# A mixture-of-experts stage in which each pair of experts shares one rest of 32 rows

## The reference

```python
g_sel = jnp.argmax(p_grp, axis=-1)
top_p, top_e = lax.top_k(jax.nn.softmax(le_sel, axis=-1), TOP_K)      # TOP_K = 2
e_idx = g_sel[:, None] * E_PER_GROUP + top_e
def expert_rows(args):
    xb, e = args
    return (jax.nn.silu(xb @ w_e_gate[e]) * (xb @ w_e_up[e])) @ w_e_down[e]
contrib = ys[dest].astype(jnp.float32) * w_flat[order][:, None]
return jax.ops.segment_sum(contrib, tok_sorted, num_segments=T)
```

## Time and profile before

| | us |
|---|---|
| median of the runs | 2455.64 (2447.79 to 2460.75) |
| profiled execution, its own time | 2455.0 |
| its span on the core | 2455.0 |
| PE busy | 2273.7 (93%) |
| PEld busy | 1570.4 (64%) |
| DVE busy | 1204.2 (49%) |
| ACT busy | 822.2 (33%) |
| POOL busy | 119.8 (5%) |
| HBM read and written | 384.10 MB and 16.83 MB, 163 GB/s over the span |

### The profile page before, as it was taken

How to read it: one execution, slowest core, us unless ns; L and a number is a source line. 1 busy time by engine, 2 the same in 40 slices (tenths; PEclk the granted TensorE clock), 3 DMA queues, 4 the chain that set the end, 5 groups by cost and what they waited for, 6 DMA issues and landing times.

```text
span 2455.0 us, 29702 instructions
## 1 busy us (share of the span) xinstructions
PE 2273.7 (93%) x11726; PEld 1570.4 (64%) x11726; DVE 1204.2 (49%) x1761; ACT 822.2 (33%) x1255; POOL 119.8 (5%) x160
## 2 busy tenths in 40 slices
PE   6999998679999999978997689999999889999997
PEld 3788756423333333346777677888887777888885
DVE  3799576400000000047756543877824473877922
ACT  3322453311111111135474164332424273323422
POOL 0000000021111111100003000000000000000000
PEclk8999999889999999988999589999999899999999
DMA  8442204539999999831120011222222301222221
GB/s 354 184 170 77 82 15 191 220 122 380 385 381 382 389 388 389 324 143 69 69 102 2 1 35 69 103 103 103 103 103 80 127 1 69 103 92 83 99 103 69
DMA packets 36406, 384.56 MB, mean 157 GB/s; under 512 B 10080, under 2 KB 10336, under 8 KB 13408
## 3 DMA queue, kind: packets, MB, share of 16 engines
q1 hardware_dynamic: 27520, 374.91, 39.1%
q0 software_dynamic: 8800, 8.45, 1.0%
HBM read 384.10 MB, written 16.83 MB: 163 GB/s over the span
## 4 chain that ended last, share of the span: by engine, by line
PE 69%; DVE 5%; ACT 3%; issue 1%; DMA 1%; POOL 0%; SPq 0%; DVEq 0%; ACTq 0%; POOLq 0%
PE PS L616 14%; PE PS L618 14%; PE PS L617 14%; PE PS L818 9%; PE PS L857 5%; PE PS L838 5%; PE PS L865 2%; PE PS L988 1%; PE PS L808 1%; PE PS L576 1%; PE PS L1181 0%; PE PS L903 0%; DVE A L1812 0%; DVE A L2412 0%; DMA A<-y_assignments 0%
## 5 line engine op out<-in xcount | busy, mean ns | idle before, releaser
L616 PE MATMUL PS<-h_hi_r,w_hi_r 128*128 128x512 f32 x1056 | 425.1, 403 | 11.8 <-DVE A L1812 5.0
L617 PE MATMUL PS<-h_r,w_hi_r 128*128 128x512 f32 x1104 | 433.8, 393 | 0.0
L618 PE MATMUL PS<-h_hi_r,ring_r 128*128 128x512 f32 x1056 | 414.5, 392 | 0.0
L2084 DVE TENSOR_TENSOR ring_r<-ring,w_hi_r 128x1024 fp32r<-128x1024 f32 x196 | 238.7, 1222 | 341.6 <-ACT w_hi_r L1424 341.5
L1424 ACT ACTIVATE w_hi_r<-ring 128x1024 fp32r<-128x1024 f32 x196 | 206.1, 1057 | 462.7 <-PE PS L618 292.0
L616 PEld LDWEIGHTS PS<-h_hi_r,w_hi_r 128*128 128x128 f32 x1056 | 200.5, 190 | 66.6 <-issue 12.7
L617 PEld LDWEIGHTS PS<-h_r,w_hi_r 128*128 128x128 f32 x1104 | 210.2, 190 | 47.3 <-issue 4.8
L618 PEld LDWEIGHTS PS<-h_hi_r,ring_r 128*128 128x128 f32 x1056 | 200.5, 190 | 42.7
L2073 DVE TENSOR_TENSOR A<-A,PS 128x512 f32<-128x512 f32 x16 | 11.0, 688 | 395.9 <-PE PS L818 395.9
L818 PE MATMUL PS<-A 128*64 128x512 f32 x768 | 170.2, 600 | 0.1
L1812 DVE SCALAR_TENSOR_TENSOR A<-A,vec 128x511 f32<-128x511 f32 (+15 forms) x216 | 160.1, 741 | 6.7
(11 more groups left out here) (463 smaller groups left out, 3622.5 us busy)
## 6 DMA issues: line engine op xcount, KB each, us to landing
A<-wexp SPq DMA_DIRECT2D x64, 2048.0 KB, 9.4
ring<-wall SPq DMA_DIRECT2D x63, 2048.0 KB, 8.0
ring<-wexp SPq DMA_DIRECT2D x16, 2048.0 KB, 17.0
h<-wexp SPq DMA_DIRECT2D x16, 2048.0 KB, 13.3
A<-wada SPq DMA_DIRECT2D x12, 2048.0 KB, 15.8
x<-xt_in SPq DMA_DIRECT2D x2, 2048.0 KB, 11.6
A<-y_assignments SPq DMA_DIRECT2D x4, 1024.0 KB, 8.0
h_tokens<-A SPq DMA_DIRECT2D x4, 512.0 KB, 2.8
```

Of the source, the lines that this page charges most:

```text
L616: mm(out, w[0], x_[0], start=first, stop=False)
L617: mm(out, w[0], x_[1], start=False, stop=False)
L618: return mm(out, w[1], x_[0], start=False, stop=last_)
L2084: tt(ring_r[:, slot, :, cols], ring[:, slot, :, cols], w_hi_r[:, :, cols].bitcast(F32), ALU.subtract).then_inc(S("w_lo"), 1)
```

## The change

Per pair there is now one rest of 32 rows instead of two. It belongs to the expert of the pair with more rows; the kernel works out from the counts which one that is and puts it first (`place` in the routing, a table `blki` that is no longer the identity). So the first expert of a pair has room for 96 rows, the second for 64. In the first two pairs (FIXED) the order stays, because their gates are loaded before the counts are known. A pair has 160 slots instead of 192, and the additional pairs hold 160 rows of one expert.

The rest's products keep their number, and each has 256 columns: the four column groups of the array take (gate, up) x (half of the 512 columns) of the one expert for gate and up, and a quarter of the 1024 output columns each for down. Gate and up use columns 0 to 255 of PSUM bank 5, down columns 256 to 511. The hidden rest is 64 partitions (two halves) x 256, and is turned in two transposes. The results leave PSUM in four copies of 32x256.

On the SP queue the loop now reads six experts at its head, and per pair it issues ups(p) and gates(p+1) together at the end of the rest of gate and up of p-1, and downs(p) at the end of the rest of down of p-1. The last downs are issued behind the loop, when the copies of the last pair but one are done.

```diff
-PAIR_ROWS = 2 * CAP
+PAIR_ROWS = 2 * HALF + QUARTER
+FIXED = 2
-MORE = 2 * T // (CAP + 1)
+MORE = 2 * (2 * T // (CAP + 1 + HALF + 1))
...
-                for q in range(2):
-                    es = [expert(2 * d + q, j) for j in range(2)]
-                    rwait(sp, S("m_pc"), 2 * PRODUCTS * d + m_done(q - 2, 2))
-                    for j in range(2):
-                        gate_of(q, j, es[j])
-                    rwait(sp, S("m_pc"), 2 * PRODUCTS * d + m_done(q - 1, 2))
-                    for j in range(2):
-                        up_of(j, es[j])
-                    rwait(sp, S("m_pc"), 2 * PRODUCTS * d + m_done(q - 1, 4))
-                    for j in range(2):
-                        down_of(j, es[j])
+                done = 2 * PRODUCTS * d
+                before, first, second = experts(2 * d - 1), experts(2 * d), experts(2 * d + 1)
+                gates(0, first)
+                rwait(sp, S("m_pc"), done + m_done(-2, 4))
+                downs(before)
+                rwait(sp, S("m_pc"), done + m_done(-1, 2))
+                ups(first)
+                gates(1, second)
+                rwait(sp, S("m_pc"), done + m_done(-1, 4))
+                downs(first)
+                rwait(sp, S("m_pc"), done + m_done(0, 2))
+                ups(second)
+            rwait(sp, S("m_y1"), 2 * n)
+            downs(experts(2 * n - 1))
...
-                        for part, w in enumerate((moe_gate[q], moe_up)):
-                            for j in range(2):
-                                r = HALF * part + QUARTER * j
-                                last = mm(PS[r:r + QUARTER, 5, :], x_rest[:, k * HALF + QUARTER * j:k * HALF + QUARTER * (j + 1)], w[j][:, k, :],
-                                          start=k == 0, stop=k == KD - 1)
+                        for t in range(4):
+                            w = (moe_gate[q], moe_up)[t // 2][0]
+                            last = mm(PS[QUARTER * t:QUARTER * (t + 1), 5, 0:256], x_rest[:, k * QUARTER:(k + 1) * QUARTER],
+                                      w[:, k, 256 * (t % 2):256 * (t % 2 + 1)], start=k == 0, stop=k == KD - 1)
...
-                    pe.wait_ge(S("m_h"), 4 * d + (2 * q + 2))
-                    for k in range(4):
-                        last = nc.tensor.transpose(PS[:, 4, k * P:(k + 1) * P], A[:, 48, k * P:(k + 1) * P], ident)
+                    rwait(pe, S("m_h"), 4 * d + (2 * q + 2))
+                    for k in range(2):
+                        last = nc.tensor.transpose(PS[:, 4, k * HALF:(k + 1) * HALF], hid_rest[:, k * P:(k + 1) * P], ident[0:HALF, 0:HALF])
...
-                        for half in range(2):
-                            for j in range(2):
-                                r = HALF * half + QUARTER * j
-                                last = mm(PS[r:r + QUARTER, 5, :], hT_rest[:, k * HALF + QUARTER * j:k * HALF + QUARTER * (j + 1)],
-                                          moe_dn[j][:, 4 * half + k, :], start=k == 0, stop=k == 3)
+                        at = HALF * (k % 2) + QUARTER * (k // 2)
+                        for t in range(4):
+                            last = mm(PS[QUARTER * t:QUARTER * (t + 1), 5, 256:512], hT_rest[:, at:at + QUARTER],
+                                      moe_dn[0][:, 4 * (t // 2) + k, 256 * (t % 2):256 * (t % 2 + 1)], start=k == 0, stop=k == 3)
...
-                    for half in range(2):
-                        last = a_(yb[1][:, half, :], PS[HALF * half:HALF * (half + 1), 5, :], ACT.Copy)
+                    for t in range(4):
+                        last = a_(yb[1][:, t // 2, 256 * (t % 2):256 * (t % 2 + 1)], PS[QUARTER * t:QUARTER * (t + 1), 5, 256:512], ACT.Copy)
...
-            link(ts(er[1], er[0], float(CAP), None, ALU.is_gt))
-            for rows_in in range(CAP + PAIR_ROWS, T, PAIR_ROWS):
-                link(stt(er[1], er[0], float(rows_in), er[1], ALU.is_gt, ALU.add))
+            link(tt(place[:, :, 0], count[:, :, 1], count[:, :, 0], ALU.is_gt))
+            link(nc.vector.memset(place[:, 0:FIXED, 0], 0.0))
+            link(ts(place[:, :, 1], place[:, :, 0], -1.0, 1.0, ALU.mult, ALU.add))
+            link(ts(er[6], er[2], -float(QUARTER), float(CAP), ALU.mult, ALU.add))
+            link(tt(er[7], er[0], er[6], ALU.subtract))
+            link(ts(er[1], er[7], 0.0, None, ALU.is_gt))
+            for rows_in in range(PAIR_ROWS, T - HALF, PAIR_ROWS):
+                link(stt(er[1], er[7], float(rows_in), er[1], ALU.is_gt, ALU.add))
...
+            link(stt(er[5], er[2], -float(QUARTER), er[5], ALU.mult, ALU.add))
+            link(stt(er[3], er[2], float(HALF), C("slot0"), ALU.mult, ALU.add))
-            link(tt(asg[3], rank, by_expert(C("slot0")), ALU.add))
-            link(stt(asg[4], rank, float(HALF), by_expert(C("slot1")), ALU.is_ge, ALU.mult))
+            link(tt(asg[3], rank, by_expert(er[3]), ALU.add))
+            link(ts(asg[4], rank, float(HALF), float(HALF), ALU.is_ge, ALU.mult))
             link(tt(asg[3], asg[3], asg[4], ALU.add))
-            link(stt(asg[4], rank, float(CAP), by_expert(er[5]), ALU.is_ge, ALU.mult))
+            link(tt(asg[4], rank, by_expert(er[6]), ALU.is_ge))
+            link(tt(asg[4], asg[4], by_expert(er[5]), ALU.mult))
...
-            rows_of = (P, HALF)
+            rows_of = (P, QUARTER)
```

More of the change, by code:

```diff
@@ L73 @@
 CONSTS = [("ident", P), ("ones", P), ("after", P), ("tri_strict", P), ("tri_incl", P),
-          ("iota4", NG), ("iota8", EPG), ("iotab", MORE), ("iotae", E), ("slot0", E), ("slot1", E), ("slot2", E)]
+          ("iota4", NG), ("iota8", EPG), ("iotab", MORE), ("iotap", E), ("slot0", E), ("slot2", E)]
 COFF, NCST = {}, 0
@@ L240, in build @@
         lgT = rstd[:]
-        er = [carve(E) for _ in range(6)]
+        er = [carve(E) for _ in range(8)]
         blk = carve(MORE, E)
@@ L294, in build @@
         moe_gate = [[A[:, 8:16], A[:, 16:24]], [ring[:, 0], ring[:, 1]]]
[L295 to L299, removed]
+        xg = [A[:, 40:42, :], A[0:QUARTER, 42:44, :]]
+        x_main, x_rest = A[:, 44:46, :], A[:, 46, 0:KD * QUARTER]
+        hid_main, hid_rest = A[:, 47, :], A[0:HALF, 48, 0:256]
+        hT_main, hT_rest = A[:, 49, :], A[:, 50, 0:2 * HALF]
+        yb = [A[:, 51:53, :], A[0:QUARTER, 53:55, :]]
         DOUBLES_MIN, DOUBLES_MAX = PAIRS // 2, -(-PAIRS_ALL // 2)
@@ L477, in _, with experts, downs, gates @@
                 up_of(j, wexp[2 + j:3 + j])
-            for j in range(2):
-                sp.wait_ge(S("m_pc"), m_done(0, 4))
-                down_of(j, wexp[2 + j:3 + j])
             n = doubles(sp)
-            def expert(i, j):
-                e = sp.value_load(blki[0:1, bass.ds(2 * i + j, 1)], min_val=0, max_val=E - 1)
-                return wexp[bass.ds(e, 1)]
-            with sp.Fori(1, n) as d:
-                for q in range(2):
-                    es = [expert(2 * d + q, j) for j in range(2)]
-                    rwait(sp, S("m_pc"), 2 * PRODUCTS * d + m_done(q - 2, 2))
-                    for j in range(2):
-                        gate_of(q, j, es[j])
-                    rwait(sp, S("m_pc"), 2 * PRODUCTS * d + m_done(q - 1, 2))
-                    for j in range(2):
-                        up_of(j, es[j])
-                    rwait(sp, S("m_pc"), 2 * PRODUCTS * d + m_done(q - 1, 4))
-                    for j in range(2):
-                        down_of(j, es[j])
+            def experts(pair):
+                return [wexp[bass.ds(sp.value_load(blki[0:1, bass.ds(2 * pair + j, 1)], min_val=0, max_val=E - 1), 1)] for j in range(2)]
+            def downs(es):
+                for j in range(2):
+                    down_of(j, es[j])
+            def gates(q, es):
+                for j in range(2):
+                    gate_of(q, j, es[j])
+            def ups(es):
+                for j in range(2):
+                    up_of(j, es[j])
+            with sp.Fori(1, n) as d:
+                done = 2 * PRODUCTS * d
[12 more added lines that the diff above has]
+            downs(experts(2 * n - 1))
             rwait(sp, S("m_sg"), 4 * n)
@@ L810, in rows_T @@
                 for k in range(KD):
-                    last = nc.tensor.transpose(PS[:, 2, k * HALF:(k + 1) * HALF], xg[1][:, k // 4, (k % 4) * P:(k % 4 + 1) * P], ident[0:HALF, 0:HALF])
+                    last = nc.tensor.transpose(PS[:, 2, k * QUARTER:(k + 1) * QUARTER], xg[1][:, k // 4, (k % 4) * P:(k % 4 + 1) * P], ident[0:QUARTER, 0:QUARTER])
                 last.then_inc(S("m_tr"), 1)
@@ L1394, in rows_out @@
                 act.wait_ge(S("m_tr"), count + 1)
-                a_(x_rest, PS[:, 2, :], ACT.Copy).then_inc(S("m_x"), 1)
+                a_(x_rest, PS[:, 2, 0:KD * QUARTER], ACT.Copy).then_inc(S("m_x"), 1)
             rows_out(1)
@@ L1403, in _ @@
                     act.wait_ge(S("m_pc"), done + m_done(q, 2))
-                    a_(hid_rest, PS[0:HALF, 5, :], ACT.Silu).then_inc(S("m_sg"), 1)
+                    a_(hid_rest, PS[0:HALF, 5, 0:256], ACT.Silu).then_inc(S("m_sg"), 1)
```

(19 more changed lines are left out.)

3 lines of the change are left out of this document (1 added, 2 removed).

## The result

The changed kernel takes 2420.07 us (median of four, 2416.55 to 2429.3) against 2452.97 for the kernel before (four runs, with one more than the three ahead of the prediction): a ratio of 0.9879, interval 0.9859 to 0.9899, 33 us less. The profiled execution has a span of 2414.8 us, at the low end of the four. The prediction said 2413, range 2396 to 2438.

The account below looks back on a forecast made before the run. The prediction took TensorE to bound the old expert stage and transfers the new one, at 31.8 us a pair. From 2455.0 us: -40.8 (stage) - 3.5 (first rest) + 1.8 + 0.4 = -42.1, giving 2413 us, range 2396 to 2438.

Parts of the forecast that it names:

- The bound before: Expert stage of the kernel before: TensorE sets 34.16 us a pair, transfers need 31.96, only 2.2 us less.
- The rests at half cost, 28.5 us of need: Expert stage: rests fall from 7.00 and 3.57 us to 3.50 and 1.79; TensorE's need is 28.52 us a pair.
- Placing of rows +1.8: Ahead of the stage: the VectorE chain that places the rows gets more small operations, 1.8 us added.
- Behind the stage +0.4: After the stage: last copies are four of 32x256 instead of two of 64x512, between 0 and 1.2, taken as 0.4 us.
- The pair at 31.8: Expert stage after the change: bound by transfers at 31.8 us a pair, chance 0.71.
- This holds only if the queue never runs dry: SP weight queue: next ups issued 5.6 us before the queue's end, start from standstill costs 2.4, so slack is 3.2.
- The signs of being wrong: Changed profile: wait before rest rows' transposes, gap in DMA row, rests over 6.8 us, or more than sixteen pairs.
- The rival of the late gather: Next pair's second gather lands at 22.8 us after the pair's end, costing 1.5 us in 14 pairs: 2434; chance 0.10.
- The clock: TensorE's clock may fall to half behind the new 3.3 us wait: 1.7 us in the last pair, up to 4.
- The rate: Rival: weight transfers run at 422 GB/s or more throughout, 31.0 us a pair, 2402 us; chance 0.10.
- More blocks: Rival: one expert over its room makes two more pairs run, 64 us, 2477 us; chance 0.02.
- The range: Whole kernel: 2396 to 2438 us, from 400 GB/s (13 more), clock 4 and run-to-run spread 5, reaching further for the gather.

Follow-up runs that it names:

- before_new_order: The kernel before with the changed SP order alone (ups of p and gates of p+1 together, then downs of p): 2449.18 us, pair 34.18.
- before_early: The kernel before with the gather for pair i+2 issued ahead of the scatters of pair i, nothing else: 2453.0 us (one run), pair 34.16.
- half_loads: The changed kernel with loop loads bringing only half the bytes of each weight: 2365.19 us (one run), pair 28.69.
- early_old_order: The changed kernel with the gather issued ahead of the scatters and the SP order of the kernel before: 2402.46 us, ratio 0.9799 to the kernel before.
- gather_early: The changed kernel with the gather for pair i+2 issued ahead of the scatters of pair i: 2415.82 us, ratio 0.9832 to the kernel before.
- old_order: The changed kernel with the SP queue's order of the kernel before: 2447.52 us, ratio 0.9975 to the kernel before, pair 34.51.
- early_old_warm: The changed kernel with early gather, the kernel before's SP order, and three unused products ahead of TensorE's wait for the ups: 2406.59 us.

## Why the prediction was right, and where it was not

*The bound before* (TensorE, 34.16 a pair, transfers close behind): right. before_new_order and before_early leave the pair at 34.18 and 34.16, half_loads shows 28.69 once transfers are light.

*The rests at half cost, 28.5 us of need*: right, 28.69; each rest 0.07 to 0.09 above the half.

*Placing of rows +1.8*: right, 8.7 for 7.0. *Behind the stage +0.4*: it was +1.8, within what two executions differ by.

*The pair at 31.8*: the kind of bound was right in part, the term was mis-sized. From the first to the fifteenth pair's main down the changed kernel took 454.13 us, 32.44 a pair, 0.64 x 14 = 9 us over the forecast; this is the whole gap of the third line of the table. The step that failed is "This holds only if the queue never runs dry". I worked out 3.2 us of slack for the ups and counted 1.7 us for a fall of the clock, as something "which the wait of the next pair absorbs". A fall cost twice that: 2.3 or 1.7 us on main down (9.31, 8.71 for 7.02) and up to 1.6 on the turning (1.94 + 0.99 + 0.40 for 0.87 + 0.61 + 0.26), on top of a wait of 2.1 to 3.0 for the gather. Eight of the fourteen pairs have such a fall at their start, and in exactly these eight the queue ran low (a DMA share under 0.6) for 0.6 to 3.1 us before the ups were issued, 16 us in all. The transfers show 373 to 408 GB/s in these eight pairs and 419 to 426 in the other six.

Two errors stand against each other in this term. Over the fourteen pairs the changed kernel shows 405 GB/s at a DMA share of 0.97, so 405 / 0.97 = 418 when the queue is full, and early_old_order shows 418 at 1.00. By an estimate from these numbers a queue that never ran dry would have given 454.13 x 0.97 / 14 = 31.5 us, less than the 31.8 that I had from 411. The forecast's rate was too low and its queue too full, and that the pair came out only 0.64 off is partly luck.

*The signs of being wrong.* Two that I had named came true although the time lies in the range: TensorE's wait stands before the turning and not before main down, and the transfers have gaps.

*The rival of the late gather*, chance 0.10, had the mechanism: gathers land a median of 14.4 us after issue (13.0 before) and 15.8 at most. In the pair shown the second lands 20.7 after the pair's end (issued 797.18, pair's end 792.05). I had set the point from which it costs at 21.3, because the downs would land at 23.0; they landed at 20.5 (issued 792.81, landed 19.7 later), since the queue ran faster there than the 411 that I had taken. So the two arrive together, the wait stands before the turning (25.7 us in 13 waits in the stage) and not before main down, and the turning comes on top. It costs 0.4 us a pair by gather_early (32.19 to 31.80), which the medians don't part from nothing.

*The clock* I had taken as a matter of 0 to 4 us. For the changed kernel the runs show some 6 us, not told apart from nothing; with the old order, where all sixteen pairs but the first and the last have a fall, the falls cost 34 us, which I hadn't thought possible. I had also held the queue's order to be a detail to be followed; without it, and with the gather as it is, the change is worth 3 us.

*The rate.* 422 GB/s or more throughout, chance 0.10, would have given 2402, and that is where early_old_order ended, with 419: the rate was nearly there, the changed kernel's schedule didn't use it. The weighing of the Trainium skill's page (HBM Reference, Specifications) comes out for its second figure: about 425 GB/s for a core alone, and the traces show 424 to 426 over whole pairs (419 in the mean of early_old_order's stage); its 358 is no limit here.

*More blocks*: 64 foretold, 61 measured.

*The range.* Its upper sum, 2413 + 13 + 4 + 5, is 2435 and not 2433; nothing hangs on it.

## What to carry to other kernels

When a bound is lifted and the next one is 2 us behind it, follow every chain that spans the step, not the largest only: here the weights (31), the gathered rows (20.7 + turning + down) and the queue's lead had nearly the same length, and whichever waits first hits the others. Work that waits for nothing should not stand in an in-order queue behind work that does: moving the gather ahead of the scatters made the fastest kernel of all, 2402 us, with the simpler order of weights. And a short wait on TensorE can cost more than its length, because what follows may run at half clock; test it by filling the wait.

## What the runs showed of the hardware that I had not expected

In the changed kernel's stage TensorE's clock fell to 0.50 eight times, each time around a wait of 2.1 to 3.0 us for the gather with 0.6 us of transposes ahead of it and about 2 behind it. It stayed there for 6.8 us, once for 3.4. Two waits of 1.6 and 1.8 us in the same place had no fall. With the old order all fourteen waits, 1.9 to 3.7 us long, had one, of 6.8 or 10.2 us; in early_old_order four waits of 1.9 us ahead of the ups had none. The kernel before has the same transposes, no wait and no fall. The stretch ahead of such a fall and the one behind it, with the old order:

```profile
796.00:799.40 3.40, 0.13 (x2) 0.02 (x1) 0.42 (x1) 0.60 (x1) 0.00 (x0) 0.96 1.00 416
799.40:805.00 5.60, 5.59 (x24) 3.53 (x26) 0.29 (x1) 1.37 (x2) 0.00 (x0) 0.50 1.03 436
```

TensorE was busy 0.13 of 3.4 us, then at 0.50 of its clock. The Trainium skill (TensorE: Matmul & The Clock Gate, "Loop structure matters more than you think") describes this, a long wait on a transfer between matmuls after which the engine runs cold; the trace agrees, with shorter waits. It shows in addition that a fall can cost about as much again as the wait before it (34 us over fourteen falls in old_order, 2.4 us each, behind 39.0 us of waits), through a transfer queue that is left empty, or nothing that the runs can show where the queue stays full (early_old_warm).
